# Sparse attention: who clears head 0's queries, and where the convolution's norm and the values' low halves stand

## The reference

```
(a_val, a_gate, b_gate, c_gate, b_h, q, k, v, q_idx, k_idx, w_idx) = split(rms_norm(x) @ w_in)
y_a = silu(layer_norm(causal_dwconv(a_val * sigmoid(a_gate), 31 taps) + dw_b))   # 256 channels
y_b = b_gate * causal_dwconv(c_gate * b_h, 3 taps)                               # 256 channels
y_c = sparse attention: an indexer picks 128 keys for each query by top-k; 8 heads of 64;
      softmax over the picked keys, in blocks of 128 queries
x = x + concat(y_a, y_b, y_c) @ w_out
```

## Time and profile before

| | |
|---|---|
| time, median of 3 runs | 3659.76 us (3655.61 to 3665.55) |
| span of the profiled execution | 3669.0 us |
| TensorE busy | 3517.8 us, 96% of the span |
| VectorE busy | 2031.0 us, 55% |
| ScalarE busy | 991.7 us, 27% |
| GpSimd busy | 2013.0 us, 55% |
| chain that ended last | PE 78%, DVE 11%, issue 4%, ACT 3%, POOL 2% |

### The profile page before, as it was taken

How to read it: one execution, slowest core, us unless ns; L and a number is a source line. 1 busy time by engine, 2 the same in 40 slices (tenths; PEclk the granted TensorE clock), 3 DMA queues, 4 the chain that set the end, 5 groups by cost and what they waited for, 6 DMA issues and landing times.

```text
span 3669.0 us, 44368 instructions
## 1 busy us (share of the span) xinstructions
PE 3517.8 (96%) x16768; PEld 2891.8 (79%) x16768; DVE 2031.0 (55%) x2964; ACT 991.7 (27%) x1714; POOL 2013.0 (55%) x1209
## 2 busy tenths in 40 slices
PE   8999997989999999999898999999999999999998
PEld 6888775878888888877687888877878887778887
DVE  5554597736552455249872655257576525767631
ACT  2111146232110111014623211015432203543210
POOL 5666465336666666646433666641266663236664
PEclk9999998999999999999899999999999999999999
DMA  3323271312223323327231223345122335412232
GB/s 131 96 95 95 93 187 47 114 59 92 98 96 95 98 97 96 97 93 184 58 114 58 93 98 96 95 137 129 41 92 98 95 98 148 118 50 94 94 96 86
DMA packets 106684, 362.43 MB, mean 99 GB/s; under 512 B 14304, under 2 KB 14720, under 8 KB 105856
## 3 DMA queue, kind: packets, MB, share of 16 engines
q1 hardware_dynamic: 91648, 319.41, 27.3%
q0 software_dynamic: 8640, 31.46, 4.6%
q10 hardware_dynamic: 6208, 8.92, 0.9%
HBM read 317.27 MB, written 2.10 MB: 87 GB/s over the span
## 4 chain that ended last, share of the span: by engine, by line
PE 78%; DVE 11%; issue 4%; ACT 3%; POOL 2%; DMA 1%; ACTq 1%; DVEq 0%; SPq 0%; POOLq 0%
PE banks L564 26%; PE banks L565 25%; PE banks L566 25%; DMA w_raw<-mid 1%; DVE h_lo L925 1%; PE banks L987 1%; DVE square_sum L688 1%; DVE bias L1631 1%; DVE conv_acc L1656 1%; DVE diagonals L1656 1%; POOL qz_even_hi L1300 1%; DVE w_lo L605 1%; DVE best L1627 1%; POOL w_hi L600 0%; PE banks L807 0%
## 5 line engine op out<-in xcount | busy, mean ns | idle before, releaser
L605 POOL TENSOR_TENSOR w_lo<-w_raw,w_hi 128x1024 fp32r<-128x1024 f32 (+1 forms) x508 | 1248.8, 2458 | 40.7
L600 POOL CAST w_hi<-w_raw 128x1024 fp32r<-128x1024 f32 (+1 forms) x540 | 564.9, 1046 | 1252.3 <-PE banks L566 1167.9
L564 PE MATMUL banks<-h_hi,w_hi 128*128 128x512 f32 x2928 | 1157.1, 395 | 41.4 <-DVE h_lo L925 13.5
L565 PE MATMUL banks<-h_lo,w_hi 128*128 128x512 f32 x2928 | 1146.3, 391 | 0.0
L566 PE MATMUL banks<-h_hi,w_lo 128*128 128x512 f32 x2928 | 1145.7, 391 | 0.0
L564 PEld LDWEIGHTS banks<-h_hi,w_hi 128*128 128x128 f32 x2928 | 553.6, 189 | 171.5 <-issue 33.8
L566 PEld LDWEIGHTS banks<-h_hi,w_lo 128*128 128x128 f32 x2928 | 553.4, 189 | 117.5
L565 PEld LDWEIGHTS banks<-h_lo,w_hi 128*128 128x128 f32 x2928 | 554.0, 189 | 111.9
L564 PE MATMUL banks<-act_hi,w_hi 128*128 128x512 f32 x1056 | 411.1, 389 | 0.9 <-DVE x L966 0.9
L566 PE MATMUL banks<-act_hi,w_lo 128*128 128x512 f32 x1056 | 410.8, 389 | 0.0
L565 PE MATMUL banks<-act_lo,w_hi 128*128 128x512 f32 x1056 | 410.8, 389 | 0.0
(11 more groups left out here) (432 smaller groups left out, 4552.1 us busy)
## 6 DMA issues: line engine op xcount, KB each, us to landing
w_raw<-gu SPq DMA_DIRECT2D x176, 512.0 KB, 3.5
w_raw<-mid SPq DMA_DIRECT2D x120, 512.0 KB, 3.5
w_raw<-up SPq DMA_DIRECT2D x88, 512.0 KB, 3.5
w_raw<-dn SPq DMA_DIRECT2D x96, 448.0 KB, 3.3
w_raw<-mix SPq DMA_DIRECT2D x62, 512.0 KB, 3.5
w_lo<-w_raw POOLq DMA_DIRECT2D x50, 512.0 KB, 5.1
w_raw<-dn SPq DMA_DIRECT2D x48, 512.0 KB, 3.5
w_raw_third<-mid SPq DMA_DIRECT2D x10, 512.0 KB, 5.4
```

The source lines that it names most:

```text
L564: pe.matmul(out, w_hi, m_hi, start=start, stop=False, skip_group_check=True)
L565: pe.matmul(out, w_hi, m_lo, start=False, stop=False, skip_group_check=True)
L600: g.tensor_copy(wh[:, ch.slot, 0:width], raw_tile(ch, width)).then_inc(Ring.hi[ch.slot], 1)
L605: eng.tensor_tensor(wl[:, ch.slot, 0:width], raw_tile(ch, width), f32(wh[:, ch.slot, 0:width]), ALU.subtract).then_inc(Ring.split[ch.slot], 1)
```

## The change

ScalarE clears head 0's queries, in two activations after the split of chunk 24 and ahead of the splits of chunks 25 and 26. GpSimd clears heads 1 to 7; head 1 now comes after chunk 26, heads 2 to 4 after chunk 27. ScalarE's split of chunk 27 moves from ahead of the attention into step 6. The high halves of the values are made in the order of blocks 2, 0, 1, 3; their low halves are spread over VectorE's step 0 (one, ahead of it) and steps 1, 3 and 4. The deviations move behind item 1 on VectorE (step 2), their squares behind item 1 on ScalarE, and the low parts of `y_b` into steps 3 and 4. A table set that holds both Ln and Exp is loaded once, ahead of the attention. Two waits of TensorE follow the values' low halves.

```diff
@@ signals, mix1_pe
-    qz_s = sig("q_padded", 2 * HEADS)
+    qz_s, qz_first_s = sig("q_padded", 2 * (HEADS - 1)), sig("q_padded_first", 2)
             if h == 0 and t == 2:
-                pe.wait_ge(v_lo_s.sem, v_lo_s(l, T))
-            if t == 0:
-                pe.wait_ge(qz_s.sem, qz_s(l, 2 * (h + 1)))
+                pe.wait_ge(v_lo_s.sem, v_lo_s(l, 1))
+            if h == 0 and t == 0:
+                pe.wait_ge(qz_first_s.sem, qz_first_s(l, 2))
+            elif t == 0:
+                pe.wait_ge(qz_s.sem, qz_s(l, 2 * h))
         def outputs(h):
+            if h == 0:
+                pe.wait_ge(v_lo_s.sem, v_lo_s(l, T))
@@ GpSimd
-    PADDED_AT = {V_CHUNK + 3: (0, 1), OUT_CHUNK + 2: (1, 5), OUT_CHUNK + 3: (5, 6), OUT_CHUNK + 4: (6, HEADS)}
+    PADDED_AT = {OUT_CHUNK + 1: (1, 2), OUT_CHUNK + 2: (2, 5), OUT_CHUNK + 3: (5, 6), OUT_CHUNK + 4: (6, HEADS)}
+    V_ORDER = (2, 0, 1, 3)
@@ mix1_act
-        for m in range(V_CHUNK + 3, OUT_CHUNK + 2):
+        own_split(V_CHUNK + 3)
+        act.wait_ge(prope.sem, prope(l, 10))
+        act.wait_ge(short_s.sem, short_s(l, 11))
+        for tile, full in ((qz_hi, qk_hi), (qz_lo, qk_lo)):
+            act.activation(tile[0][:, :], f32(full[:, 4, :]), ACT.Copy, scale=halfcol[:, 0:1]).then_inc(qz_first_s.sem, 1)
+        for m in range(OUT_CHUNK, OUT_CHUNK + 2):
             own_split(m)
-        for t in range(T):
+        for t in V_ORDER:
...
-        own_split(OUT_CHUNK + 2)
-        for k in range(2):
-            act.wait_ge(ln_dev.sem, ln_dev(l, k + 1))
-            act.activation(dev_sq[:, k, :], dev[:, k, :], ACT.Square).then_inc(ln_sq.sem, 1)
+        act.preload_act_table_set("natural_log_exp_and_others")
         def conv_norm(s):
-            if s == 3:
+            if s == 1:
+                for k in range(2):
+                    act.wait_ge(ln_dev.sem, ln_dev(l, k + 1))
+                    act.activation(dev_sq[:, k, :], dev[:, k, :], ACT.Square).then_inc(ln_sq.sem, 1)
+            elif s == 3:
...
+            elif s == 6:
+                own_split(OUT_CHUNK + 2)
@@ mix1_dve
-        for t in range(T):
-            v.wait_ge(v_hi_s.sem, v_hi_s(l, t + 1))
+        def value_low(i):
+            t = V_ORDER[i]
+            v.wait_ge(v_hi_s.sem, v_hi_s(l, i + 1))
             v.scalar_tensor_tensor(v_lo[:, t, :], bank[4 + t][:, :], st[:, 2, t:t + 1], f32(v_hi[:, t, :]),
...
+        value_low(0)
...
         def conv_norm(s):
+            if s == 1:
+                value_low(1)
+            elif s == 2:
+                v.wait_ge(ln_mean.sem, ln_mean(l, 1))
+                for k in range(2):
+                    v.scalar_tensor_tensor(dev[:, k, :], bank[2][:, :], -1.0 / 256, acc[:, k, :], ALU.mult, ALU.add)\
+                        .then_inc(ln_dev.sem, 1)
+            if s in (3, 4):
+                value_low(s - 1)
+                yab_low(s - 3, s - 1)
```

More of the change, by code:

```diff
@@ L1659, in mix1_dve @@
         v.wait_ge(conv1.sem, conv1(l, 2 * CONVW + 2))
-        for t in range(T):
-            v.wait_ge(v_hi_s.sem, v_hi_s(l, t + 1))
+        def value_low(i):
+            t = V_ORDER[i]
+            v.wait_ge(v_hi_s.sem, v_hi_s(l, i + 1))
             v.scalar_tensor_tensor(v_lo[:, t, :], bank[4 + t][:, :], st[:, 2, t:t + 1], f32(v_hi[:, t, :]),
                                    ALU.mult, ALU.subtract).then_inc(v_lo_s.sem, 1)
-        v.wait_ge(ln_mean.sem, ln_mean(l, 1))
-        for k in range(2):
-            v.scalar_tensor_tensor(dev[:, k, :], bank[2][:, :], -1.0 / 256, acc[:, k, :], ALU.mult, ALU.add)\
-                .then_inc(ln_dev.sem, 1)
+        value_low(0)
         def yab_low(i, k):
@@ L1673, in yab_low @@
                 .then_inc(yab_lo.sem, 1)
-        for i, k in enumerate((2, 3)):
-            yab_low(i, k)
         def conv_norm(s):
+            if s == 1:
[8 more added lines that the diff above has]
+                yab_low(s - 3, s - 1)
             if s == 3:
```

## The result

The changed kernel takes 3668.08 us, median of 20 runs (3660.02 to 3672.62); the kernel before took 3659.14 us in 20 runs beside it (3648.53 to 3668.5). The ratio is 1.0025, with a 95% interval of 1.0017 to 1.0032: it is slower by about 9 us (6 to 12), which is under the 0.3% that the prediction took as its bound. The forecast was 5.9 us.

The account below looks back on a forecast made before the run. The prediction took TensorE's idle time as the bound. Layer 1's +7.4 us and layer 0's -1.5 us sum to +5.9, put on the median 3659.76 for 3665.7 us, range 3650 to 3677.

Parts of the forecast that it names:

- The wait that the prediction put at the centre: TensorE idles some 10 us before head 2's first score, its clear queued behind chunk 27's DMA and ScalarE's late split.
- The other signs: Layer 0's first score directly follows the last product, no GpSimd clear is near 17 us, Ln and Exp have no load between.
- The steps of the estimate: From y_a's high parts: 2.45 us to the split, DMA 0.29 after it taking 0.85, two clears at 1.56 each.
- The gain in layer 0: Layer 0's output projection starts at 590.7 against 592.19, 1.5 us won, the new wait nearly using up the stalls' 8.9.
- The first two stalls: TensorE's waits of 5.20 and 6.54 us at layer 0's attention start, worth 8.9 us in layer 0 only.
- Head 1's first score: In both layers it stays 10.9 us after the convolution ends, the chain from the mean to GpSimd's clears not shortened.
- rival D: VectorE's two-input steps delay head 1's clear on GpSimd: at most 3 us per layer, +11.9 us, 3671.7; chance 0.10.
- The reciprocal root: Without ScalarE's two table loads, VectorE's refinement starts 1.5 us earlier, with ends of 0.5 and 2.5 us.
- the price: Layer 1's output projection starts 7.4 us later through head 2's clear waiting for the split; ends 5.5 and 9 us.
- 2w - 11.9: Total change, w being how long head 2's clear holds the output projection behind VectorE's low parts; forecast 8.9, sign change 6.0.
- B: The 17.46 us GpSimd clear in layer 0 is an accident of the profiled execution: 14.8 us lost, 3674.6; chance 0.18.
- C: Head 2's clear on GpSimd isn't late, so both layers gain: -11.9 us, 3647.9; chance 0.12.

Follow-up runs that it names:

- The first experiment: The changed kernel with GpSimd's clear of head 2's queries moved ahead of chunk 27's adding DMA: 3652.21 us, ratio 0.9979 to the kernel before.
- the fourth: The kernel before with chunk 27's split in step 6 and head 1's clear ahead of that chunk's DMA: 3674.59 us, ratio 1.0043.
- the third experiment: The kernel before with only head 0's clear moved from GpSimd to ScalarE: 3652.27 us, ratio 0.9975.
- two table sets: The changed kernel with head 2 cleared ahead of chunk 27's DMA and without the table preload, so Ln and Exp have a load each: 3651.15 us, ratio 0.9972.
- head 1 on ScalarE: The changed kernel with head 2 cleared ahead of chunk 27's DMA and head 1 cleared by ScalarE in step 2: 3647.28 us, ratio 0.9966.
- clear earlier: The kernel before with GpSimd's clear of head 0 behind chunk 22's DMA instead of chunk 24's: 3654.41 us, ratio 0.9981.
- clear and set: The kernel before with head 0 cleared by ScalarE and one table set preloaded behind chunk 27's split: 3652.67 us, ratio 0.9978.
- lows later: From head 1 on ScalarE: the values' fourth low half and two low parts of y_b moved to VectorE's step 6; 3647.49 us, ratio 0.9965.
- the second experiment: The changed kernel with chunk 27's split back ahead of the attention, before the table load: 3658.91 us, ratio 0.9993 to the kernel before.

## Why the prediction was right

**The sign and the mechanism.** The wait that the prediction put at the centre is there: in both layers, 10.46 us where it said "some 10", ended by GpSimd's low tile of head 2, with the DMA and the split ahead of it in that order. The first experiment takes it away with one number and the fourth brings it in with the late split alone. The other signs are there too: the first scores have no wait, the longest clear on GpSimd after is 2.27 us, and Ln and Exp follow each other without a load (567.35 and 567.99 in layer 0).

**Its length.** From VectorE's first low half to the output projection I forecast 32.6 us. In layer 0 after it is 590.13 - 557.64 = 32.5, in layer 1 1778.50 - 1747.17 = 31.3. Against before that is -1.6 us in layer 0 (forecast -1.5) and +6.1 in layer 1 (forecast +7.4). The steps of the estimate, by layer 0: ScalarE spent 2.41 us (580.42 to 582.83) between the high parts of `y_a` and the split (2.45 forecast), the DMA went 0.29 us behind the split (0.29), the clear began 0.65 us after the DMA (0.85), and two clears ended 3.42 us later (3.1). In layer 0 the terms err in both directions and by less than half a microsecond each.

**The gain in layer 0.** The first two stalls go: of the waits of the earlier trace rows the first is gone in the trace after and the second is down to 0.92 us, and the third experiment times them at 9 us (4 to 15), where the prediction had 8.9. Layer 0's output projection starts 2.1 us earlier by the profile, 1.5 forecast.

**Head 1's first score.** Forecast 10.9 us behind the convolution; 569.06 - 557.64 = 11.4 in layer 0, 1757.78 - 1747.17 = 10.6 in layer 1. GpSimd's pair took 4.3 and 4.0 us against 3.7 in the earlier trace rows. That is rival D in small, 0.3 to 0.6 us and not the 3 of D's bound. VectorE's run is broken there by steps on PSUM and by waits, as the prediction argued; no run tests that this is what keeps it small.

**The reciprocal root.** VectorE's refinement starts without a wait in both layers:

```profile
571.72 0.69 DVE L731 TENSOR_TENSOR conv_norm<-conv_norm 128x512 f32<-128x512 f32 x1
...
1760.09 0.68 DVE L731 TENSOR_TENSOR conv_norm<-conv_norm 128x512 f32<-128x512 f32 x1
```

That is 14.1 and 12.9 us behind the first low half's start; before, in layer 1, it was 1770.35 - 1754.81 = 15.5. So it comes 1.4 us earlier in layer 0 and 2.6 in layer 1, where 1.5 was forecast with ends of 0.5 and 2.5. The 1.1 us too little in layer 1 is most of the 1.3 by which the price there was set too high.

**Where it is off by 3 us.** The timed difference is 9 us with an interval of 6 to 12, and the forecast of 5.9 lies at its lower edge; the two stretches of the traces give +4.6. Laid side by side, the ten kernels show where the rest is (both stretches together, and the time, each less the kernel before; us):

| kernel | stretches | time |
|---|---|---|
| after | +4.6 | +9.1 |
| head 2 first | -12.9 | -7.7 |
| split back | -4.1 | -2.6 |
| clear only | -10.4 | -9.1 |
| split only | +12.3 | +15.7 |
| two table sets | -12.3 | -10.2 |
| head 1 on ScalarE | -15.1 | -12.4 |
| clear earlier | -9.3 | -7.0 |
| clear and set | -11.8 | -8.1 |
| lows later | -17.4 | -12.8 |

The times follow the stretches one to one (a straight line through the ten has a slope of 1.0), and every one lies above them, by 1.3 to 5.2 us and 3.1 on average. So a microsecond in these stretches is a microsecond of time, and nothing sets the refinement's apart. What is off is most likely what all ten have in common, the one profile of the kernel before. In the prediction's sum 2w - 11.9 the likeliest term to be too large is therefore the 8.9 us for layer 0's stalls, read from that execution, by some 3 us; head 2's wait and the refinement are as forecast or better. The spread of the timed runs fits this: the 35 runs of the kernel before beside the first four experiments lie between 3648.1 and 3674.6 us, the 12 of the third experiment between 3648.5 and 3656.2, and 8 of the 35 are no slower than the slowest of those. So the stalls may well cost much in some executions and little in others. The third experiment alone, with 4 to 15 us, can't choose between 8.9 and 6, and there is no profile of an execution of before without the long clear in layer 0: whether it is this term, or something outside the two stretches, stays open. The forecast owes some of its nearness to two errors that go against each other, a price 1.3 us too high in layer 1 and a gain likely some 3 us too high in layer 0.

**The rivals.** B, the clear as an accident of one execution, falls by the third experiment, and by the fourth, whose profile has the long clear again. C had the right sign for a case that this kernel isn't: with head 2 in time the kernel is 7.7 us faster (3 to 13), where C said 11.9. D is there at a tenth to a fifth of its bound. What the prediction did not see is why the split had been moved at all: the second experiment shows that in the new order of VectorE and ScalarE a split ahead of the attention costs some 5 us. The mistake of the change is not the late split but that GpSimd's queue was left as it was, with one clear behind its DMA.

## What to carry to other kernels

When work is moved on an engine that works in order, follow who waits for it, and then what stands behind that waiter on its own queue: here a split moved on ScalarE, a DMA on GpSimd waited for it, and a clear behind the DMA held TensorE 10.46 us in each layer, though the clear had nothing to do with the split. The repair is then a place in the third engine's queue, and no run shows a cost of it. And before a profile's span is compared with another, cut it at instructions that both have: here the stretches that the change never touched differed by 8.7 us, about as much as the timed effect, and with the other sign. Where there are several experiments, lay what the traces give beside what the runs give: an offset that all share lies most likely in what they share, here the single profile of the kernel before.

## What the hardware showed that I had not expected

- A GpSimd clear with an unbroken run of VectorE's two-input steps beside it lasted until the run paused in four places: 17.46, 17.58, 6.01 and 5.66 us, against 1.55 to 1.56 alone. Moving it did not avoid that, but it made the next pause nearer. In layer 1 of the kernel before it got in at once, in 1.90 us in the middle of the same convolution, and there VectorE's next step took 1.21 us instead of 0.75 (the row below). Which it will be is repeated by layer over the two profiles with this order (long in layer 0, short in layer 1); I have no row that says why.

```profile
1737.16 1.21 DVE L1656 SCALAR_TENSOR_TENSOR diagonals<-conv_in,params,diagonals 128x512 f32<-128x512 f32 x1
```

- Once the clear gets in at a pause, VectorE pays instead, one step of 1.06 us instead of 0.69.
- ScalarE's pair for the same clear takes 1.3 us beside VectorE's convolution (539.11 to 540.43), where GpSimd takes at least 3.1.
